# A three-stage transformer kernel on one core: bias columns and weighted inputs from PSUM, a bank handed on later, all squares of six norms summed on VectorE

## The reference

```python
h = h + 0.5 * swiglu(rmsnorm(h, ffn1_norm), ffn1_w_gate_up, ffn1_w_down)
u = rmsnorm(h, mix_norm)
a_b, a_c, a_v, z, xbc, dt_raw, g_a, g_b = split(u @ w_in)
y_a = (a_b * causal_dwconv(a_c * a_v, conv_a_w)) @ w_out_a
y_b = mamba2_branch(z, xbc, dt_raw, ...)
h = h + (sigmoid(g_a) * y_a + sigmoid(g_b) * y_b) @ w_mix_out
h = h + cross_attention(rmsnorm(h, xattn_norm), rmsnorm(mem, mem_norm), ...)
h = h + 0.5 * swiglu(rmsnorm(h, ffn2_norm), ...)
out = rmsnorm(h, final_norm)

def rmsnorm(x, g): return x * rsqrt(mean(x * x) + EPS) * g
# in mamba2_branch (4 groups of 8 heads, 2 chunks of 128 tokens):
xbc = silu(causal_dwconv(xbc, conv_w) + conv_b)      # 4 taps, 24 blocks of 128 channels
x = xh * dt                                          # input of the chunked recurrence
states = einsum(bm, exp(acs[-1] - acs), x)           # state at the end of a chunk
```

## Time and profile before

| what | value |
|---|---|
| median of 3 runs | 1292.72 us (1289.46 to 1292.73) |
| profiled execution, its own time | 1293.33 us |
| its span, first to last instruction | 1291.5 us |
| mean granted clock of TensorE | 0.993 of full speed |
| TensorE busy | 97% of the span, 9023 matmul records |
| VectorE, ScalarE, GpSimd busy | 50%, 55%, 76% |
| DMA | 208.9 MB, mean 162 GB/s |

### The profile page before, as it was taken

The page is one execution under the profiler, slowest core; times in us unless marked ns, Lnnn a source line. Parts: engine busy times, 40 slices in busy tenths (PEclk is TensorE's granted clock), DMA queues, the critical chain, the costliest instruction groups (busy, mean ns, idle before and its releaser), DMA issues.

```text
span 1291.5 us, 22633 instructions
## 1 busy us (share of the span) xinstructions
PE 1255.8 (97%) x9023; PEld 1151.8 (89%) x9023; DVE 641.6 (50%) x1488; ACT 706.4 (55%) x1323; POOL 984.7 (76%) x774
## 2 busy tenths in 40 slices
PE   6999999999999999999999999999999999999997
PEld 5988899988899888889999988989999988888886
DVE  5566755557656444411857577742024334444312
ACT  5454656455556666555554565664447445666532
POOL 4655668766669999889798766678888757899894
PEclk9999999999999999999999999999999999999999
DMA  7443445444346666666465444445556535666662
GB/s 239 132 129 117 131 132 178 148 145 150 115 131 197 187 187 186 190 181 192 143 201 181 145 126 139 131 132 172 183 182 215 163 115 160 184 192 183 179 194 82
DMA packets 57784, 208.92 MB, mean 162 GB/s; under 512 B 6352, under 2 KB 7632, under 8 KB 57424
## 3 DMA queue, kind: packets, MB, share of 16 engines
q1 hardware_dynamic: 57680, 207.48, 53.4%
HBM read 206.41 MB, written 1.05 MB: 161 GB/s over the span
## 4 chain that ended last, share of the span: by engine, by line
PE 87%; DVE 8%; ACT 2%; issue 1%; DMA 0%; SPq 0%; DVEq 0%
PE bank L382 21%; PE bank L355 16%; PE bank L357 15%; PE bank L356 15%; PE bank L385 11%; PE bank L907 1%; DVE ar L1706 1%; PE bank L696 1%; DVE ar L968 1%; PE bank L2167 1%; PE bank L2139 1%; PE bank L2189 1%; PE bank L2141 1%; ACT whi L307 1%; PE bank L2140 1%
## 5 line engine op out<-in xcount | busy, mean ns | idle before, releaser
L315 POOL TENSOR_TENSOR wlo<-raw,whi 128x512 fp32r<-128x512 f32 x770 | 984.5, 1308 | 291.2 <-ACT whi L307 289.6
L307 ACT ACTIVATE whi<-raw 128x1024 fp32r<-128x1024 f32 x387 | 404.8, 1053 | 41.5 <-DMA raw<-w_dram 14.0
L355 PE MATMUL bank<-xx,whi 128*128 128x256 f32 (+1 forms) x1296 | 380.4, 293 | 13.3 <-DVE xx L445 10.3
L357 PE MATMUL bank<-xx,wlo 128*128 128x256 f32 (+1 forms) x1296 | 369.4, 285 | 0.0
L356 PE MATMUL bank<-xx,whi 128*128 128x256 f32 (+1 forms) x1296 | 369.2, 285 | 0.0
L355 PEld LDWEIGHTS bank<-xx,whi 128*128 128x128 f32 x1296 | 247.5, 191 | 22.6 <-issue 12.6
L356 PEld LDWEIGHTS bank<-xx,whi 128*128 128x128 f32 x1296 | 247.2, 191 | 0.5
L357 PEld LDWEIGHTS bank<-xx,wlo 128*128 128x128 f32 x1296 | 247.5, 191 | 0.0
L382 PE MATMUL bank<-xx,whi 128*128 128x512 f32 x704 | 178.9, 396 | 0.0
L355 PE MATMUL bank<-yy,whi 128*128 128x256 f32 (+1 forms) x524 | 151.2, 289 | 0.0
L357 PE MATMUL bank<-yy,wlo 128*128 128x256 f32 (+1 forms) x524 | 148.9, 284 | 0.0
(11 more groups left out here) (273 smaller groups left out, 1456.2 us busy)
## 6 DMA issues: line engine op xcount, KB each, us to landing
raw<-w_dram SPq DMA_DIRECT2D x387, 512.0 KB, 3.7
h<-x_dram SPq DMA_DIRECT2D x2, 544.0 KB, 6.9
cst<-con_dram SPq DMA_DIRECT2D x1, 1049.0 KB, 10.9
ar<-mem_dram SPq DMA_DIRECT2D x1, 1024.0 KB, 7.4
out_dram<-h SPq DMA_DIRECT2D x4, 256.0 KB, 2.5
cst<-con_dram SPq DMA_DIRECT2D x1, 134.0 KB, 3.6
prm<-par_dram SPq DMA_DIRECT2D x1, 131.0 KB, 3.5
```

Of the source, the lines that this page charges most:

```text
L307: e.activation(whi[:, i % NSPL, :], raw[:, i % NRAW, :], ACT.Copy).then_inc(*whi_done.done(i))
L315: return e.tensor_tensor(wlo[:, q, c0:c1], raw[:, i % NRAW, c0:c1], whi[:, q, c0:c1].bitcast(F), ALU.subtract)
L355: e.matmul(o, wh, both[:, 0, :], start=(i == 0), stop=False)
L357: m = e.matmul(o, wl, both[:, 0, :], start=False, stop=(i == len(feed) - 1))
```

## The change

It has four parts.

1. In six norms (`last` = 7: all but n0 and fin) VectorE also adds the eighth square, and TensorE's second set of sums falls away. The words that announce the change speak of five; by the rule in the code n1, f1, mx, x, f2 and mem are meant. The first set now waits for the seventh addition.
2. The bias columns of the convolution are computed from the block's PSUM bank (bank x 0 + bias) instead of copied from the parameters, behind the wait for the block's product.
3. `xw` is computed from the transposed input in PSUM with a factor `dtde` (dt x decay, one new small product), ahead of both `xdt` products instead of behind them. The negated cumulative sums (`negA`) are read from PSUM too.
4. In groups 0 to 2 the bank of the normalizing row is given back not when it is taken, but in the next group, once the state product has taken its bank.

```diff
@@ class Norm
+EARLY_SUMS = ("n0", "fin")
+        self.last = 6 if key in EARLY_SUMS else 7
@@ norm_begin, norm_square, norm_add
-        side_.give(("acc", N.key), (v_step, ("acc", N.key, 6)))
+        side_.give(("acc", N.key), (v_step, ("acc", N.key, N.last)))
-        sqb.give(("sq", N.key, c), (v_step, ("acc", N.key, c)) if c < 7 else (piece, ("sums", N.key)))
+        sqb.give(("sq", N.key, c), (v_step, ("acc", N.key, c)) if c <= N.last else (piece, ("sums", N.key)))
-        e.tensor_tensor(acc_of(N) if c < 6 else row_of(N), acc_of(N), sqb.at("sq", N.key, c)[:, N.c0:N.n],
+        e.tensor_tensor(acc_of(N) if c < N.last else row_of(N), acc_of(N), sqb.at("sq", N.key, c)[:, N.c0:N.n],
@@ norm_sums
-                e.wait_ge(*v_step.of("acc", N.key, 6))
+                e.wait_ge(*v_step.of("acc", N.key, N.last))
...
-        for j, (t0, n) in enumerate(N.tiles):
+        for j, (t0, n) in enumerate(N.tiles if N.last < 7 else []):
             if j == 0:
                 e.wait_ge(*s_step.of("sq", N.key, 7))
@@ residuals_vector
+        if N.last == 7:
+            norm_add(e, N, 7)
@@ steps_vector
-        e.tensor_scalar(negA, tokm[:, 2:4, :], -1.0, None, ALU.mult).then_inc(*v_step.done("negA"))
+        o = side_.at("dtT")
+        e.tensor_scalar(negA, o[:, 64:128].rearrange("p (a b) -> p a b", b=32), -1.0, None, ALU.mult).then_inc(
+            *v_step.done("negA"))
+        e.tensor_tensor(dtde, o[:, 128:160], tokm[:, 0, :], ALU.mult).then_inc(*v_step.done("dtde"))
@@ taps
-            e.tensor_copy(s[:, 0:3], cbh[:, cb:cb + 1].broadcast_to([128, 3])).then_inc(*v_step.done("bias", cb))
...
                 if i == 0:
                     e.wait_ge(*product.of("cv", cb))
+                    e.tensor_scalar(s[:, 0:d], o[:, 0:d], 0.0, cbh[:, cb:cb + 1], ALU.mult, ALU.add).then_inc(
+                        *v_step.done("bias", cb))
@@ ssd_tensor
         e.matmul(o, btok, xw, start=True, stop=True).then_inc(*piece.done("st", g))
+        if held:
+            held.pop()()
...
         o = side_.take(e, "gr", g)
-        side_.give(("gr", g), (v_step, ("yn", 4 * g + 3)))
+        give = lambda: side_.give(("gr", g), (v_step, ("yn", 4 * g + 3)))
+        held.append(give) if g < 3 else give()
@@ ssd_vector
+        deb = dtde[:, hs].unsqueeze(2).broadcast_to([128, 8, 64])
+        e.wait_ge(*piece.of("xT", g, 0))
+        e.wait_ge(*v_step.of("dtde"))
+        e.tensor_tensor(xw.rearrange("p (h q) -> p h q", q=64), side_.at("xT", g, 0).rearrange("p (h q) -> p h q", q=64),
+                        deb, ALU.mult).then_inc(*v_step.done("xw", g))
...
-        deb = tokm[:, 4, hs].unsqueeze(2).broadcast_to([128, 8, 64])
-        e.wait_ge(*v_step.of("xdt", g, 0))
-        e.tensor_tensor(xw.rearrange("p (h q) -> p h q", q=64), xdt[:, 0, :].rearrange("p (h q) -> p h q", q=64), deb,
-                        ALU.mult).then_inc(*v_step.done("xw", g))
@@ cross_vector, memory norm
-                if 0 < c < 7:
+                if c:
                     norm_add(e, NM, c)
```

More of the change, by code:

```diff
@@ L477, in norm_sums @@
         side_.give(("sums", N.key), (v_step, ("rstd", N.key, len(N.parts) - 1)))
-        last = sqb.at("sq", N.key, 7)
         for j, (t0, n) in enumerate(N.tiles):
             if j == 0:
-                e.wait_ge(*v_step.of("acc", N.key, 6))
-            e.matmul(b[0:n, j:j + 1], N.row[:, t0:t0 + n], ones[:, 0:1], start=(j == 0), stop=False,
-                     skip_group_check=True)
-        for j, (t0, n) in enumerate(N.tiles):
+                e.wait_ge(*v_step.of("acc", N.key, N.last))
+            m = e.matmul(b[0:n, j:j + 1], N.row[:, t0:t0 + n], ones[:, 0:1], start=(j == 0), stop=(N.last == 7),
+                         skip_group_check=True)
+        for j, (t0, n) in enumerate(N.tiles if N.last < 7 else []):
             if j == 0:
                 e.wait_ge(*s_step.of("sq", N.key, 7))
-            m = e.matmul(b[0:n, j:j + 1], last[:, t0:t0 + n], ones[:, 0:1], start=False, stop=True,
+            m = e.matmul(b[0:n, j:j + 1], sqb.at("sq", N.key, 7)[:, t0:t0 + n], ones[:, 0:1], start=False, stop=True,
                          skip_group_check=True)
@@ L1501, in ffn_scalar @@
         residuals_scalar(e, K.nxt)
-    (zacc, xs0, xs1, bc0, bc1, zs0, zs1, xdt, btok, xw, prev, M, E8, cv0, cv1, cv2, mt0, mt1, mt2, tokm, negA, acol) = arena(
+    (zacc, xs0, xs1, bc0, bc1, zs0, zs1, xdt, btok, xw, prev, M, E8, cv0, cv1, cv2, mt0, mt1, mt2, tokm, negA, dtde, acol) = arena(
         (8, S), (4, S), (4, S), (2, S), (2, S), (4, S), (4, S), (2, 512), (128,), (512,), (512,), (8, 256),
-        (8, 128), (S,), (S,), (S,), (S,), (S,), (S,), (5, 32), (2, 32), (1,))
+        (8, 128), (S,), (S,), (S,), (S,), (S,), (S,), (5, 32), (2, 32), (32,), (1,))
     xsT, BC, zs = [xs0, xs1], [bc0, bc1], [zs0, zs1]
@@ L1571, in steps_tensor @@
         o = side_.take(e, "dtT")
-        side_.give(("dtT",), (s_step, ("tokm",)))
+        side_.give(("dtT",), (v_step, ("dtde",)))
         e.wait_ge(*s_step.of("dden"))
@@ L1703, in taps @@
         for cb in cbs:
-            s = cv.take(e, cb)
+            cv.take(e, cb)
             cv.give((cb,), (v_out, ("cv", cb)))
-            e.tensor_copy(s[:, 0:3], cbh[:, cb:cb + 1].broadcast_to([128, 3])).then_inc(*v_step.done("bias", cb))
         for i in range(3):
@@ L1740, in silu_vector @@
                 *v_step.done("cvx", cb))
+    held = []
     def ssd_tensor(e, g):
```

## The result

The changed kernel took 1281.49 us (median of 4 runs, 1279.67 to 1283.42), the kernel before 1291.78 on the same chip (4 runs, 1289.46 to 1292.73). The ratio is 0.9923, with its interval 0.9902 to 0.9944: faster by 10 us, between 7 and 13. The forecast was 1283.5, with a range of 1280 to 1288. The same kernel again, beside the later experiments: 1280.34 (5 runs, 1279.6 to 1282.84), ratio 0.9926 [0.9912, 0.9939].

The account below looks back on a forecast made before the run. TensorE, busy 97% of the span, was taken as the bound. Bias columns 4.0 + bank wait 4.0 + norms 2.4 - 0.6 = 9.8 us off the profiled 1293.33 gives 1283.5 us, range 1280 to 1288.

Parts of the forecast that it names:

- The bias columns: First convolution pair: bias from PSUM removes a 2.42 us TensorE stall and 1.60 us of low clock behind it, 4.0 us.
- The slack: First convolution pair: channel block 16's bank free at 692.5, TensorE needing it at 693.78, so 1.3 us and no wait.
- That PSUM operands cost more: Moved VectorE instructions: the skill's figures would give 1.8 us more VectorE time for 28; the trace was read as the reverse.
- The weighted inputs and the bank: State product in groups 1 to 3: TensorE's 1.33 us wait for the row's bank goes, three times, 4.0 us.
- heir of the wait: Recurrence groups: no later segment was found to take over the bank's wait once the row's bank is handed on later.
- the other 22 bias copies: Remaining convolution blocks: no TensorE wait hangs on these copies, so they count nothing; at worst 8 us of VectorE time.
- The norms: Six norms: second sets of sums matmuls gone, 2.4 us off TensorE, less 0.6 us of new waits for the additions.
- The bound of 1.5 us for the waits: Six norms' sums: upper bound of the new waits, if a weight load that has to wait costs 0.15 more at each.
- The first: Rival, first convolution pair: copy's stall partly chance, term 2 us or less; a still-late block gives 1286 to 1287.5; chance 0.2.
- The second: Rival, state products: the bank's three waits return at the first or second segment, 1.3 us each, 1287.5 us; chance 0.08.
- The third, the slow side: Rival, six norms: late additions stall TensorE over 2 us, each paying 4.0 us, 13.6 slower, 1307 us; chance 0.03.
- The fourth: Rival, mixer's end: other chains take back the middle's gains, leaving only the norms, 1291 us; chance 0.06.

Follow-up runs that it names:

- e2: Changed kernel with the bias copied from SBUF again, at the new instruction's place behind the wait for the product: 1289.4 us, ratio 0.9994 to the kernel before.
- e5: Kernel before with the norms' part of the change alone: 1289.74 us, ratio 0.9994 to the kernel before.
- e8: Changed kernel with the bias computed ahead of the wait as a product of two SBUF inputs (bias x ones): 1287.42 us, ratio 0.9971 to the kernel before.
- e1: Changed kernel with the bias copied from SBUF again, ahead of the wait for the product: 1286.11 us, ratio 0.9966 to the kernel before.
- e6: Kernel before with only the later hand-on of the normalizing row's bank: 1286.32 us, ratio 0.9968 to the kernel before.
- e3: Changed kernel with the row's bank given back at once, weighted input still computed from PSUM: 1282.32 us, ratio 0.9941 to the kernel before.

## Why the prediction was right, step by step

**The bias columns, forecast 4.0: 4.0 in the two traces.** Stall 2.42 and low clock 1.60, at their place. The op took 0.21 us where I took 0.2. The slack was larger than I gave: channel block 16 is free when the first of the two L1749 ends, at 687.18 + 0.42 = 687.60, which with the lead of 4.2 us is 691.8 in the time of the earlier trace rows, where I said 692.5: 2.0 us ahead of need and not 1.3. One reading was wrong without harm: the queue had 30 splits and not ten. And one thing was taken for fixed that isn't: the low clock behind the stall is there in the profiles of before, e2, e5 and e8, and not in e1 and e6. The part is worth 2.4 to 4.0 us, by execution, so that the whole 4.0 is right for the profile it was read from and would be some luck for another. An estimate for the mean, with four of six: 2.4 + 1.6 x 4/6 = 3.5 us.

**That PSUM operands cost more.** Where nothing is in the way, 3 columns took 158 ns from SBUF and 210 from PSUM, 52 more. The Trainium skill, "Perfetto Trace Analysis", on optimizing Scalar/DVE operations, has 65 more (125 against 60). The trace agrees as to the sign; the sizes can't be set side by side closely, since the two are different operations and the Trainium skill says there that its figures are busy times, of which profiled latency is about twice. Under GpSimd's load the order turns round, 8.4 us against 0.2, and 1.77 against 0.69 for a 128x512 product. The Trainium skill, "GPSIMD Engine Reference", Key points, has GpSimd contend with VectorE instructions in a 2-port mode or with two SBUF inputs. e8, with two SBUF inputs, agrees; the copy waited as long, and no run shows in which mode it ran. Why at this place the whole queue has to empty stays open. In the six traces with SBUF-only bias instructions 51 of these took over 0.18 us, and each ended 0.02 to 0.03 us behind the end of a split; but beyond the first pair none took over 1.34 us, that is, they passed between two splits. One of them in e2, VectorE's timeline:

```profile
728.70 1.11 DVE L1721 COPY ar<-prm 128x3 f32<-128x3 f32 x1
```

GpSimd's:

```profile
728.50 2.53 POOL L320 TENSOR_TENSOR wlo<-raw,whi 128x512 fp32r<-128x512 f32 x2 [0.63 <-ACT whi L312]
```

The copy ends at 729.81, about where the second split begins (728.50 + 2.53/2 = 729.77), and not at 731.03.

**The weighted inputs and the bank, forecast 4.0: 4.0, and 0.6 beside it.** Three steps of 1.32 to 1.33 us, as worked out from the earlier trace rows. No heir of the wait, as argued: 850 to 960 us has no stop of TensorE either. I had named the bank as the cause and the faster product as hidden; the first is right (e6: gone, with L1835 unchanged), the second only in that order. Taken alone the faster product would have brought all but 0.24 us of each wait (e3). The 0.6 us were not in the sum: I had said that on the other 22 bias copies no wait of TensorE hangs. None is listed in the earlier trace rows, but small delays of banks do: with the copies back, e1 loses 0.5 us in two steps at 777 and 816.

**The norms, forecast 2.4 less 0.6: 2.0.** TensorE at the sums of f1 in the changed kernel, against the earlier trace rows:

```profile
420.99 0.28 PE L390 MATMUL bank<-xx,wlo 128*128 128x256 f32 x1
421.19 0.61 PE L486 MATMUL bank<-cst,rows 128*128 128x1 f32 x4
421.66 1.64 PE L387 MATMUL bank<-xx,whi 128*128 128x512 f32 x6
```

The last projection matmul hands over after 0.12 us, at 421.11; the sums start at 421.19, so the new addition costs 0.1 us, as said. From the start of the sums to the next projection matmul it is 0.47 us; with both sets it was 0.81, from 424.70 to 425.51. mem loses 0.2 us by the wait and gains 0.15 net, as said. In sum the six norms gave 2.0 us, 0.2 more than the 1.8 forecast. The bound of 1.5 us for the waits took 0.15 us more for a weight load that has to wait; no row showed that price, and f1's 0.1 has no room for it.

**Rivals.** The first (the stall partly chance) is half true: not the stall, which the profiles of all six kernels with a copy or an SBUF-only form have at this place (before, e1, e2, e5, e6, e8), but the clock behind it. Six executions show it, and not how all of them are. The second didn't come; e3 is the nearest to it, with 0.24 us a group and not 1.3. The third, the slow side, would have needed 1.7 us a norm; 0.1 to 0.2 were seen. The fourth fell with the window behind 850.

**The sum** was made against a profiled execution of 1293.33, 1.5 above the median of before shown above. 10.6 us off the median 1291.78 would be 1281.2, and 1281.49 was measured. The difference to 1283.5 is that base, and 0.8 us in the terms (10.6 against 9.8). The base alone would have put the forecast at 1282.0.

## What to carry to other kernels

When a tiny VectorE instruction takes microseconds, look at what GpSimd does until the moment it ends, in a window that is wide enough to show the whole queue. If the two ends agree, move one operand of it into PSUM (multiply a bank that is at hand by zero), and leave its place in the order alone; the SBUF-only copy moved behind the wait made it worse (e2). When TensorE waits for VectorE, ask which of its inputs is late: here the data was there and the bank wasn't, and handing on the bank a step later, with no instruction changed, removed the whole wait, where the faster product alone left 0.24 us of each. Of a stall, count the granted clock behind it as a second term that may or may not come, so give it as a range.

## What the runs showed of the hardware that was not expected

- A VectorE instruction of 3 columns with both ends in SBUF lasted 6.8 to 8.4 us beside the last 6 or 7 of 30 back-to-back GpSimd splits, in either form, with one input or two. The splits kept their 1.25 us each (12.57/10 in e8, 11.29/9 in e2), so VectorE alone paid. With its source in PSUM it took 0.203 to 0.225 us, all 24 times. Elsewhere the SBUF forms were held until the end of a split too, but for 1.34 us at most.
- After the same stop of 2.2 to 2.4 us TensorE's granted clock fell to mostly the 1.2 GHz level in some executions (0.57 over 4 us in before, e2 and e8, up to 1.6 us lost) and stayed at 1.00 in others (e1, e6). The same happened at two places that no edit touches, behind stops of 1.8 us (L530, at 24 us) and 1.4 us (L930, at 319 us), which both profiles of the changed kernel have. In the second one the windows behind them are:

```profile
25.00:29.00 4.00, 4.00 (x21) 3.97 (x21) 1.72 (x5) 2.19 (x4) 2.77 (x3) 0.59 0.50 142
319.00:323.00 4.00, 3.89 (x19) 3.58 (x19) 0.70 (x3) 0.75 (x1) 2.51 (x2) 0.57 0.31 116
```

  In the first one they are at 1.00, and it was 3.2 us faster. Such steps of some 1.5 us help to keep parts of 2 us below the reach of a median here.
